# Second block: the reciprocal root as a row, sent through a line in DRAM instead of multiplied out of diagonals

## What is computed

```python
def second_block(x, ...):
    for l in range(DEPTH):                                   # DEPTH = 2
        h = swiglu_ffn(rmsnorm(x, ffn1_pre_g[l]), ffn1_w_gu[l], ffn1_w_down[l])
        x = x + 0.5 * rmsnorm(h, ffn1_post_g[l])
        h = mixing_sublayer(rmsnorm(x, mix_pre_g[l]), w_in[l], ...)
        x = x + rmsnorm(h, mix_post_g[l])
        h = swiglu_ffn(rmsnorm(x, ffn2_pre_g[l]), ffn2_w_gu[l], ffn2_w_down[l])
        x = x + 0.5 * rmsnorm(h, ffn2_post_g[l])

def rmsnorm(x, g):      # y = x * lax.rsqrt(mean(x * x, axis=-1) + EPS) * g
def swiglu_ffn(h, w_gu, w_down):     # a, b = split(h @ w_gu); (silu(a) * b) @ w_down
```

## Time and profile before

| | |
|---|---|
| three runs, us | 1901.58, 1899.76, 1900.01 |
| the profiled execution, us | 1900.14 |
| its span, us | 1898.4 |
| TensorE busy, us (share) | 1890.1 (100%) |
| VectorE busy | 1415.8 (75%) |
| ScalarE busy | 899.5 (47%) |
| GpSimd busy | 234.2 (12%) |
| mean transfer rate, GB/s | 188 |

### The profile page before, as it was taken

How to read it: one execution, slowest core, us unless ns; L and a number is a source line. 1 busy time by engine, 2 the same in 40 slices (tenths; PEclk the granted TensorE clock), 3 DMA queues, 4 the chain that set the end, 5 groups by cost and what they waited for, 6 DMA issues and landing times.

```text
span 1898.4 us, 26047 instructions
## 1 busy us (share of the span) xinstructions
PE 1890.1 (100%) x10054; PEld 1621.3 (85%) x10054; DVE 1415.8 (75%) x1629; ACT 899.5 (47%) x949; POOL 234.2 (12%) x199
## 2 busy tenths in 40 slices
PE   9999999999999999999999999999999999999998
PEld 7888888888888888888898888888888898888887
DVE  7986866579768666766779787667766779787666
ACT  6554443445544344543645545435444545545443
POOL 0000000000001000000059220000000049320000
PEclk9999999999999999999999999999999999999999
DMA  8545555564456554555444456555555454455553
GB/s 301 189 171 200 190 189 188 177 224 173 178 197 222 187 199 156 211 199 188 165 168 158 177 198 221 181 192 184 205 182 193 160 189 156 169 209 190 188 186 111
DMA packets 51619, 356.78 MB, mean 188 GB/s; under 512 B 6312, under 2 KB 6448, under 8 KB 9680
## 3 DMA queue, kind: packets, MB, share of 16 engines
q1 hardware_dynamic: 47952, 341.93, 50.5%
q0 software_dynamic: 3296, 13.67, 2.3%
q10 hardware_dynamic: 288, 0.04, 0.0%
HBM read 353.50 MB, written 2.11 MB: 187 GB/s over the span
## 4 chain that ended last, share of the span: by engine, by line
PE 97%; DVE 2%; issue 1%; DMA 0%; DVEq 0%; ACT 0%; SPq 0%; POOLq 0%; POOL 0%
PE ps L234 24%; PE ps L309 13%; PE ps L317 13%; PE ps L310 13%; PE ps L239 13%; PE ps L196 4%; PE ps L198 3%; PE ps L197 3%; PE ps L2885 1%; PE ps L2886 1%; PE ps L2890 1%; DVE w_lo L172 1%; PE ps L2620 1%; PE ps L1497 1%; PE ps L214 0%
## 5 line engine op out<-in xcount | busy, mean ns | idle before, releaser
L172 DVE TENSOR_TENSOR w_lo<-raw,w_hi 128x2048 fp32r<-128x2048 f32 x314 | 719.6, 2297 | 236.5 <-ACT w_hi L165 235.7
L165 ACT ACTIVATE w_hi<-raw 128x2048 fp32r<-128x2048 f32 x314 | 600.7, 1916 | 512.0 <-PE ps L317 241.2
L234 PE MATMUL ps<-a,w_hi 128*128 128x512 f32 x2016 | 480.1, 390 | 0.0
L234 PEld LDWEIGHTS ps<-a,w_hi 128*128 128x128 f32 x2016 | 374.3, 188 | 75.3
L239 PEld LDWEIGHTS ps<-a,w_lo 128*128 128x128 f32 x2016 | 258.5, 191 | 9.8
L239 PE MATMUL ps<-a,w_lo 128*128 128x256 f32 x2016 | 261.5, 283 | 0.0
L309 PE MATMUL ps<-w_hi,a 128*128 128x512 f32 x592 | 233.4, 394 | 0.0
L310 PE MATMUL ps<-w_hi,a 128*128 128x512 f32 x592 | 230.7, 390 | 0.0
L309 PE MATMUL ps<-w_hi,mix 128*128 128x512 f32 x576 | 225.0, 391 | 0.1
L310 PE MATMUL ps<-w_hi,mix 128*128 128x512 f32 x576 | 225.0, 391 | 0.0
L317 PE MATMUL ps<-w_lo,a 128*128 128x512 f32 x592 | 146.5, 389 | 0.0
(11 more groups left out here) (427 smaller groups left out, 2120.5 us busy)
## 6 DMA issues: line engine op xcount, KB each, us to landing
raw<-in_w_b SPq DMA_DIRECT2D x198, 1024.0 KB, 4.9
raw<-in_w_a SPq DMA_DIRECT2D x124, 1024.0 KB, 4.9
rows<-in_post_gains POOLq DMA_DIRECT2D x6, 512.0 KB, 5.1
rows<-in_rows_a POOLq DMA_DIRECT2D x2, 1028.0 KB, 8.0
raw<-in_w_a SPq DMA_DIRECT2D x4, 512.0 KB, 7.1
rows<-in_rows_a POOLq DMA_DIRECT2D x2, 1024.0 KB, 6.9
x<-in_x SPq DMA_DIRECT2D x2, 512.0 KB, 5.4
a_gates<-bias_line POOLq DMA_DIRECT2D x2, 512.0 KB, 6.8
```

The costliest lines, as they stand in the source:

```text
L165: act.activation(k.w_hi[:, s, :], k.raw[:, s, :], ACT.Copy).then_inc(k.hi_ready, 1)
L172: dve.tensor_tensor(k.w_lo[:, s, :], k.raw[:, s, :], k.w_hi[:, s, :].bitcast(F32), ALU.subtract).then_inc(k.lo_ready, 1)
L234: pe.matmul(both, hi[:, kt, n * P:(n + 1) * P], k.a[:, :, kt, :], start=kt == 0, stop=False)
```

## The change

The root is stored to a line in DRAM (256 values, token pairs interleaved: value 2p + t is partition p of tile t) and read back as a broadcast into all partitions. Both transfers are issued by ScalarE: `store_row` and `spread_row`. VectorE reads the row with a step of two elements (`r_tokens`). The diagonals, the products with ones, the copies and their waits go. The mixer's own `diag` for another purpose stays.

```diff
@@ signals and views
-        up0_done, silu0_ready, hT_done, diag_ready, rbc_done, rbc_ready = (
-            sig("up0_done", 4), sig("silu0_ready", 2), sig("hT_done", 2), sig("diag_ready", 3), sig("rbc_done", 3), sig("rbc_ready", 3))
+        up0_done, silu0_ready, hT_done, r_stored, r_spread = (
+            sig("up0_done", 2), sig("silu0_ready", 2), sig("hT_done", 2), sig("row_stored", 48), sig("row_spread", 48))
+        r_tokens = r_rows.rearrange("p (n t) -> p t n", t=TT).unsqueeze(1).broadcast_to([P, 2, TT, P])
+        by_tile = lambda v: v.rearrange("p f (t n) -> p f t n", t=TT)
+        r_line = d.bias_line[P - 1, 0, SEQ:2 * SEQ]
@@ ScalarE, new
+            def store_row(l, n):
+
+                act.wait_ge(rstd_ready.sem, rstd_ready.at(l, n + 1))
+                if l or n:
+                    act.wait_ge(r_spread.sem, r_spread.at(l, 16 * n))
+                act.dma_start(r_line.rearrange("(p t) -> p t", t=TT), rho).then_inc(r_stored.sem, 16)
+
+            def spread_row(l, n):
+
+                act.wait_ge(r_stored.sem, r_stored.at(l, 16 * (n + 1)))
+                act.dma_start(r_rows, r_line.partition_broadcast(P)).then_inc(r_spread.sem, 16)
@@ ScalarE, mlp
                 first = F0[f]
+                store_row(l, 2 * f)
                 for tt in range(TT):
...
                 split_high(k, act, st, l, first + 3)
+                spread_row(l, 2 * f)
                 split_high(k, act, st, l, first + 4)
                 if f == 0:
                     act.activation(wi_hi, wi, ACT.Copy).then_inc(wi_high.sem, 1)
-                act.wait_ge(rbc_done.sem, rbc_done.at(l, 2 * f + 1))
-                act.activation(r_rows, k.ps[:, 1, 0:SEQ], ACT.Copy).then_inc(rbc_ready.sem, 1)
@@ ScalarE, mixer
-                act.wait_ge(rstd_ready.sem, rstd_ready.at(l, 2))
+                store_row(l, 1)
...
                 high.upto(M0 + 4)
+                spread_row(l, 1)
...
-                act.wait_ge(rbc_done.sem, rbc_done.at(l, 2))
-                act.activation(r_rows, k.ps[:, 7, 0:SEQ], ACT.Copy).then_inc(rbc_ready.sem, 1)
@@ VectorE, mlp
-                for tt in range(TT):
-                    ins = dve.tensor_scalar(diag[:, tt, :], k.ident, rho[:, tt:tt + 1], None, ALU.mult)
-                ins.then_inc(diag_ready.sem, 1)
...
+                    if j == 1:
+                        dve.wait_ge(r_spread.sem, r_spread.at(l, 16 + 32 * f))
                     dve.wait_ge(asum_ready.sem, (l * 2 + f) * (FF_B - 1) + q + j)
-                    dve.tensor_tensor(r, r, mid(r_rows, 2), ALU.mult).then_inc(scaled_ready.sem, 1)
+                    dve.tensor_tensor(by_tile(r), by_tile(r), r_tokens, ALU.mult).then_inc(scaled_ready.sem, 1)
...
-                    if j == 1:
-                        dve.wait_ge(rbc_ready.sem, rbc_ready.at(l, 2 * f + 1))
@@ VectorE, mixer: the diagonals go; in evict
+                    if i == 3:
+                        dve.wait_ge(r_spread.sem, r_spread.at(l, 32))
                     dve.wait_ge(s_evicted.sem, s_evicted.at(l, i - 2))
-                    dve.tensor_tensor(scaled, scaled, mid(r_rows, scaled.shape[1]), ALU.mult).then_inc(s_scaled.sem, 1)
+                    r = r_tokens[:, 0:scaled.shape[1]]
+                    dve.tensor_tensor(by_tile(scaled), by_tile(scaled), r, ALU.mult).then_inc(s_scaled.sem, 1)
@@ TensorE, mlp
-                        pe.wait_ge(diag_ready.sem, diag_ready.at(l, 2 * f + 1))
-                        for tt in range(TT):
-                            ins = pe.matmul(k.ps[:, 1, tt * P:(tt + 1) * P], ones, diag[:, tt, :], start=True, stop=True)
-                        ins.then_inc(rbc_done.sem, 1)
...
-                pe.wait_ge(rbc_ready.sem, rbc_ready.at(l, 2 * f + 1))
@@ TensorE, mixer
-                pe.wait_ge(diag_ready.sem, diag_ready.at(l, 2))
-                for tt in range(TT):
-                    ins = pe.matmul(k.ps[:, 7, tt * P:(tt + 1) * P], ones, diag[:, tt, :], start=True, stop=True)
-                ins.then_inc(rbc_done.sem, 1)
...
-                pe.wait_ge(rbc_ready.sem, rbc_ready.at(l, 2))
```

More of the change, by code:

```diff
@@ L2365, in evict @@
                     dve.tensor_reduce(dst, halves(k, mixed_bank[i]), AX.X, ALU.add).then_inc(s_evicted.sem, 1)
+                    if i == 3:
+                        dve.wait_ge(r_spread.sem, r_spread.at(l, 32))
                     dve.wait_ge(s_evicted.sem, s_evicted.at(l, i - 2))
-                    dve.tensor_tensor(scaled, scaled, mid(r_rows, scaled.shape[1]), ALU.mult).then_inc(s_scaled.sem, 1)
+                    r = r_tokens[:, 0:scaled.shape[1]]
+                    dve.tensor_tensor(by_tile(scaled), by_tile(scaled), r, ALU.mult).then_inc(s_scaled.sem, 1)
                 hc = conv_x[:, :, CONV_PAD:]
-                dve.wait_ge(rbc_ready.sem, rbc_ready.at(l, 2))
                 evict(3, hc, hc)
@@ L2430, in _ @@
                         dve.wait_ge(k.chunk_done, st.results(l, M0 + 8))
-                        dve.tensor_tensor(qkF[:, 2:4, :], k.ps[:, mixed_bank[8], :].rearrange("p (f n) -> p f n", f=2), mid(r_rows, 2),
-                                          ALU.mult).then_inc(s_scaled.sem, 1)
+                        dve.tensor_tensor(by_tile(qkF[:, 2:4, :]), by_tile(k.ps[:, mixed_bank[8], :].rearrange("p (f n) -> p f n", f=2)),
+                                          r_tokens, ALU.mult).then_inc(s_scaled.sem, 1)
                     dve.wait_ge(ch.sem, ch.at(l))
```

## The result

| | before | after |
|---|---|---|
| median, us | 1899.98 | 1903.47 |
| range, us (runs) | 1899.47 to 1901.58 (15) | 1901.83 to 1904.93 (15) |
| the profiled execution, us | 1900.14 | 1903.76 |
| its span, us | 1898.4 | 1902.0 |

The ratio is 1.0018, with a 95% interval of 1.001 to 1.0025: 3.5 us slower. The forecast was 1898.1 with a range up to 1901.0. The median lies outside it, and next to rival 2, a late store that blocks ScalarE (1902.8).

What follows compares the result with a forecast made beforehand. TensorE, busy 100% of the span, was taken to bound the kernel. -2.35 us of removed products and +0.42 for the store's issue gave -1.93, so 1898.1 us, with a range of 1896.3 to 1901.0.

Steps and rivals of the forecast that it cites:

- rival 2: ScalarE blocked by a late store, a loss beyond about 6.3 us landing; at 8.0 us +2.8, 1902.8 us; slower: chance 0.09.
- The wait for the store: ScalarE's spread and later work wait for the store's landing: 4.0 us taken, free up to 4.3, one for one above.
- the tight place: First feed-forward pass of layer 0: down projection waits for VectorE's sum, ending an unbroken chain; later landings cost TensorE.
- TensorE, removed, and where it reaches the end: Products with ones gone: 0.45 us at three feed-forward passes, 0.50 at two mixers, all reaching the end: -2.35 us.
- the sixth place: First feed-forward pass of layer 0: TensorE arrives 0.45 us earlier and waits 0.45 us longer, gaining nothing.
- The issue on ScalarE: Store issued between root and table load: exposed 0.42 us at layer 0's first pass (bounds 0 and 0.84), nothing elsewhere.
- The spread: Broadcast of the row lands in 5.3 us, before VectorE's scaling needs it, at 771.5 against 772.5: free.
- The strided row: VectorE's scaling reads the factor with a step of two elements: 693 ns against 692 ns, cost nothing, 50 times.
- Slower: Outcome in which the change loses time, from a late store blocking ScalarE: chance 0.09, half of it within 3.8 us.
- nothing gained: Rival in which the store takes 5.6 to 6.2 us: 1899.4 to 1900.0 us; chance 0.15.

Runs made afterwards that it cites:

- e2: Kernel before, with the row made by transfers only at the first feed-forward pass of layer 0, diagonals at the other five places: 1905.13 us, ratio 1.0028.
- e3: Changed kernel plus seven unused fp32 products on TensorE ahead of its wait for the first down projection: 1901.76 us, ratio 1.001.
- v1a: Changed kernel, with ScalarE issuing the spread behind its copy of the first hidden unit in all four feed-forward passes: 1911.1 us, ratio 1.006.
- v1b: v1a, with VectorE taking the b-half's sum ahead of the scaling at the first feed-forward pass of layer 0 alone: 1906.54 us, ratio 1.0035.
- v1c: Changed kernel, with v1b's order (spread behind the hidden copy, scaling behind the b-half's sum) only at layer 0's first feed-forward pass: 1897.7 us, ratio 0.9989.
- e4: Changed kernel, with GpSimd's 512 KB gain row load held until the first place's store has landed: 1900.83 us, ratio 1.0003.
- e6a: Changed kernel, with SyncE's one 1 MB weight load beside the first place's store held until that store has landed: 1900.62 us, ratio 1.0004.
- e6b: Changed kernel, with both the gain row load and the 1 MB weight load held until the first place's store has landed: 1897.86 us, ratio 0.9991.
- e5: Changed kernel making no row at all, both transfers gone, scalings multiplying by ones, so the output is not the reference's: 1897.24 us, ratio 0.9987.
- e1: Changed kernel, with diagonals and ones again at the first feed-forward pass of layer 0, transfers at the other five places: 1898.34 us, ratio 0.999.
- v2: Changed kernel, with GpSimd issuing both transfers right behind the root; VectorE's scaling behind the b-half's sum at the first place: 1897.48 us, ratio 0.9988.

## Why the prediction was wrong

**The wait for the store: the failed step.** It took the landing as 4.0 us and free up to 4.3, each us above costing one. At the tight place it took 7.3 (and 7.2, 7.0, 7.3, 8.6, 6.8 in e2, e3, v1a, v1b, v1c). The working behind it holds: 7.3 - 4.3 = 3.0 us, with the issue's 0.42 and the 0.45 by which TensorE comes earlier, 3.87, against 3.6 by which the gap grew, and 3.8 by which the down projection moved against the transposes ahead of it. What was wrong is the size. I took it by shape from a transfer at the kernel's start and bounded it by GpSimd's two stores, without asking what runs beside this store at 762 to 770. The share of the transfer engines that I quoted, 0.76, was that of another place; at 764 to 768 in the kernel after it is

```profile
764.00:768.00 4.00, 4.00 (x28) 3.57 (x28) 0.91 (x3) 3.79 (x4) 0.41 (x1) 1.00 0.99 328
```

full. But the trace of before would not have warned me by its share either: in the same 4 us there, less the late start of 1.3 (762.7 to 766.7), it is 0.75. Its list of issues would have, with the gain row at 762.04 and a weight load at 760.92. e4, e6a and e6b show that this traffic makes most of the size: 6.1, 5.5 and 4.0 us. That e6b's 4.0 is the figure I took is luck: mine came from a load at the kernel's start.

The Trainium skill, DMA: Bandwidth & Descriptors, section "Latency and other measured facts", gives an HBM access of 0.2 us on average and 2 us at high load, and says that a lighter load makes the fixed cost smaller. The trace agrees in direction, 2.7 us alone against 7.3 beside full transfer engines, but the difference of 4.6 us is more than those two figures account for. The section that the prediction named beside its own rows, "Anatomy of one DMA" with its 2.0 us, describes transfers that GpSimd issues, and fits none of these six stores from ScalarE, of 2.7 to 7.3 us.

**A term that was not in the sum.** No step of mine, rival 2 included, asked what TensorE's clock does behind a gap. It cost 1.7 us, and e3 shows it apart from the gap. With the forecast -1.93, +3.0 for the landing and +1.7 for the clock the sum is +2.8; measured are +3.5. That rival 2 gave +2.8 too is luck, since its terms are others: of its parts only the wait at the first place (3.7 for a landing of 8.0) came; its 1.0 us at the other passes did not, and the clock stood in for it. For the profiled execution the account closes: +1.3 at the kernel's start, +5.0 at the first place, -2.7 over the rest, +3.6 in all. For the medians, +3.5, what is missing beyond +2.8 is not settled; the late start, which arises ahead of the changed part, is the likely candidate.

**TensorE, removed, and where it reaches the end: right.** In the second pass:

```profile
1159.14 0.60 PE L2675 MATMUL ps<-consts,GU 128*128 128x128 f32 x4
```

With the offset counted from the profile of before, the step at such a pass is -0.45 us, and at the first mixer -0.45 too: from the start of the weight-low products to that of the head weights' it took 2.45 us before and takes 2.00 now, so the 0.09 of the 8-row weights stayed, as the prediction had suspected, and 0.50 was a little too much. The five steps make 2.25 us; the remaining 0.4 of the 2.7 comes between 960 and 1152, behind the first mixer's place, and I have no cause for it. e5 brings 2.6 us, where 2.35 and up to 0.24 for the sixth place were expected. e1, which frees the other five, brings 1.5 where 2.35 was expected. Its profile has the late start of 1.3 us, and its faster group (1897.4 to 1897.9) lies 2.0 to 2.5 us below before; that the late start is what is missing is argued, not shown.

**The issue on ScalarE: right.** The table load's idle time grew from 1.68 to 2.07 us, by 0.39 where 0.42 stood; one issue takes 0.33 to 0.34 us. At the down projection about half of it shows: a gap of 0.6 us in e6b and v1c, which issue the store on ScalarE, against 0.4 in v2 and e5, which don't.

**The spread: right for TensorE, wrong for VectorE.** It took 4.4 to 10.4 us. In the second pass VectorE waited for it:

```profile
1164.92 0.69 DVE L2291 TENSOR_TENSOR GU<-GU,keep 128x512 f32<-128x512 f32 x1 [2.69 <-DMA keep<-bias_line]
```

and TensorE did not, because the sum of the a-half stands ahead of that wait and that of the b-half ended in time, at 1166.75, with the first product of the second half at 1167.00. v1a, with 6.11 us at the same instruction, shows where that cover ends. In the mixers ScalarE waited 1.78 and 1.35 us for the store at no cost.

**The strided row: right.**

```profile
L2291 DVE TENSOR_TENSOR GU<-GU,keep 128x512 f32<-128x512 f32 x40 | 27.7, 692 | 4.6 <-DMA keep<-bias_line 2.7 <-DVE GU L2287 0.5
```

692 ns, as in the earlier trace rows without the step.

**The chances.** "Slower" had 0.09. I had found the place, the price per us and the point (6.3 us) at which the sign turns, and had as evidence against it two landings whose surroundings I had not read. With a bound of 8.0 us measured among heavy traffic, the range had to reach it. Nor does the range follow from its own terms: "nothing gained" reaches to 1900.0, and with the 1.6 us above that is 1901.6, not 1901.0. The result lies outside even so.

## What to carry to other kernels

- A transfer that must wait for another one belongs on an engine with nothing urgent behind it: with both transfers on ScalarE the change cost 3.5 us net, and with both on GpSimd and VectorE's scaling moved back at one place it gained 2.3. Where it has to stay, put behind it only what nobody waits for, and ask what each step that it is moved past waits for.
- Price a small transfer by the traffic beside it at that moment, not by its size or the median of its kind. Here one of 1 KB landed in 2.7 to 7.3 us within one execution, and a large load beside it was late too (last section).
- A pause of TensorE is paid twice where the clock falls behind it. Where a pause can't be avoided, a few useless products in it can be worth more than they cost; here, seven fp32 ones brought back 1.7 us.

## What the runs showed of the hardware

- The 1 KB store in pieces of 8 bytes (two values of each partition) took 2.7, 2.7, 3.7, 6.6, 7.1 and 7.3 us at its six places, and 8.6 in v1b. The broadcast of that line to all partitions took 4.4 to 10.4 us, with a median of 5.9.
- A large load beside the small store is late too. GpSimd's gain row of 512 KB landed in 5.7 to 6.2 us at this place where no store stands beside it (before, e1, e5), and in 7.4 to 10.0 us in the six profiles with the store (8.6 in the kernel after). Whether the store is the cause, and by which mechanism, was not tested.
- The length of a gap alone does not tell whether TensorE's clock falls. It went to the lower level behind gaps of 3.67 us (after), 2.73 and 1.99 (both v1a) and 2.30 (v1b), and within one of 3.63 (e2); it stayed at 1.00 behind gaps of 3.07 (v1a), 2.63 (v1b) and 2.52 (e4). In e2 it fell within the gap and in the kernel after a little behind it, so that nearly equal gaps cost 2.7 and 1.7 us. That is one execution of each. The shortest gap with a fall, in v1a:

```profile
1743.13 0.50 PE L309 MATMUL ps<-w_hi,mix 128*128 128x512 f32 x1 [1.99 <-DVE GU L2300]
```

```profile
1744.00:1745.00 1.00, 1.00 (x5) 0.78 (x4) 1.00 (x1) 0.41 (x1) 0.00 (x0) 0.67 0.00 0
1745.00:1746.00 1.00, 1.00 (x4) 0.81 (x3) 1.00 (x3) 0.09 (x1) 0.00 (x0) 0.50 0.00 0
```

- Some executions start the second block 1.3 to 1.7 us later than others: the profiles of after, e1 and e6a have it, those of before, e2 and the rest do not (0.4 in v2, less in the others). It arises in the first 10 us, and the changed instructions begin only at 762. In the kernel after, TensorE's first products of `x` start 0.55 us later than in that of before, for `x` lands later, and then take nearly twice as long. First the kernel before, then after:

```profile
5.25 1.06 PE L1307 MATMUL ps<-consts,x 128*128 128x128 f32 x8 [0.20 <-DMA x<-in_x]
6.15 1.46 PE L1346 MATMUL ps<-ones 128*128 128x256 f32 x6
```

```profile
5.80 1.94 PE L1307 MATMUL ps<-consts,x 128*128 128x128 f32 x8 [0.76 <-DMA x<-in_x]
7.53 2.76 PE L1346 MATMUL ps<-ones 128*128 128x256 f32 x6
```

That is close to the ratio of the two clock levels, although the views by stretch give 1.00 there in both kernels. The trace's records of the full clock begin at 9.9 to 10.5 us in after, e1 and e6a, and at 4.4 to 7.0 us in the other ten kernels, so these starts are most likely executions in which TensorE's clock rose later; no run tests it. It fits the two groups in e1's times. Thirteen of the fifteen times of the kernel after lie at 1902.84 and above and two at 1901.83 and 1901.97, so most of them may have the late start, while two of before's fifteen lie above 1900.6. Whether it comes more often with some kernels, and so whether it carries part of the 3.5 us, stays open.
